# A diffusion step on one Trainium2 core: adaLN scale and shift brought into column form by small matmuls

## The reference

```python
def modulation(cvec, w_mod_l, b_mod_l):
    m = jax.nn.silu(cvec) @ w_mod_l + b_mod_l
    return m.reshape(cvec.shape[0], 6, D_MODEL)

def trunk_layer(x, mod, ...):
    sh1, sc1, g1, sh2, sc2, g2 = [mod[:, i][:, None, :] for i in range(6)]
    h = rms_norm(x, n1) * (1.0 + sc1) + sh1
    q, k, v, u = jnp.split(h @ w_in, ...)
    # QK norm, rotary on the sample, attention, and beside it
    # a Conformer module: gate, 31-tap convolution, layer_norm(z, ln_g, ln_b), silu
    x = x + g1 * (jnp.concatenate([attn, conv], axis=-1) @ w_out)
    h2 = rms_norm(x, n2) * (1.0 + sc2) + sh2
    x = x + g2 * grouped_moe(h2, ...)
```

## Time and profile before

| | us |
|---|---|
| median of 3 runs | 1169.36 (1165.12 to 1169.71) |
| profiled execution | 1165.68 |
| its span in the trace | 1163.8 |
| TensorE busy in it | 980.0 (84%) |
| VectorE busy | 407.9 (35%) |
| ScalarE busy | 158.2 (14%) |
| GpSimd busy | 116.8 (10%) |

### The profile page before, as it was taken

The page is one execution under the profiler, slowest core; times in us unless marked ns, Lnnn a source line. Parts: engine busy times, 40 slices in busy tenths (PEclk is TensorE's granted clock), DMA queues, the critical chain, the costliest instruction groups (busy, mean ns, idle before and its releaser), DMA issues.

```text
span 1163.8 us, 11201 instructions
## 1 busy us (share of the span) xinstructions
PE 980.0 (84%) x4106; PEld 443.5 (38%) x4106; DVE 407.9 (35%) x1072; ACT 158.2 (14%) x362; POOL 116.8 (10%) x164
## 2 busy tenths in 40 slices
PE   3589979999889988997839996999858997978890
PEld 0344525545333333333225553554523333333330
DVE  0019868733411111111042986954421111111113
ACT  0110123311000000000021023431100000000001
POOL 0100310230110000000030030041010000000001
PEclk8789979998989999998869997999769999998996
DMA  9934992348999987999975434034965999999805
GB/s 315 378 135 144 218 387 116 145 127 305 425 412 422 422 367 261 396 426 425 411 296 185 144 139 192 8 139 162 346 249 207 409 426 424 425 419 426 372 19 180
DMA packets 65412, 331.71 MB, mean 285 GB/s; under 512 B 6993, under 2 KB 9713, under 8 KB 48929
## 3 DMA queue, kind: packets, MB, share of 16 engines
q1 hardware_dynamic: 44224, 277.89, 59.9%
q10 hardware_dynamic: 12464, 23.79, 6.9%
q0 software_dynamic: 8624, 28.71, 6.8%
HBM read 308.25 MB, written 22.12 MB: 284 GB/s over the span
## 4 chain that ended last, share of the span: by engine, by line
PE 64%; DMA 19%; DVE 10%; issue 2%; ACT 2%; SPq 2%; POOL 1%; ACTq 0%; DVEq 0%; POOLq 0%
PE ps L1618 19%; PE ps L1327 15%; DMA big<-in_w_up_dram 10%; PE ps L1634 9%; PE ps L1534 7%; DVE scr L1000 4%; PE ps L1343 4%; DMA x<-in_x_sample_dram 2%; DMA big<-in_w_down_dram 2%; PE ps L1462 2%; DMA scr<-h_rows,slot_tok 1%; PE ps L1397 1%; DMA scr<-expert_rows,pick_y 1%; PE ps L1357 1%; PE ps L1602 1%
## 5 line engine op out<-in xcount | busy, mean ns | idle before, releaser
L1618 PE MATMUL ps<-big 128*64 128x512 f32 x1024 | 246.9, 633 | 41.3 <-DMA big<-in_w_up_dram 23.1
L1000 DVE SCALAR_TENSOR_TENSOR scr<-scr,convw 128x128 f32<-128x128 f32 (+1 forms) x480 | 160.5, 408 | 0.0
L1618 PEld LDWEIGHTS ps<-big 128*64 128x64 f32 x1024 | 82.0, 145 | 181.5 <-issue 167.4
L1634 PE MATMUL ps<-big,scr 128*64 128x512 f32 x624 | 146.3, 605 | 5.0 <-DVE scr L1290 4.3
L1327 PE MATMUL ps<-big 128*128 128x512 f32 (+1 forms) x384 | 146.1, 541 | 0.0
L1299 DVE TENSOR_TENSOR scr<-ps,scr 128x256 f32<-128x256 f32 x32 | 13.6, 425 | 309.9 <-ACT scr L873 309.9
L1343 PE MATMUL ps<-big,cs_rep 128*64 128x512 f32 x320 | 83.3, 667 | 22.0 <-DMA big<-in_w_mod_dram 22.0
L1327 PEld LDWEIGHTS ps<-big 128*128 128x128 f32 x384 | 72.9, 191 | 69.8 <-issue 67.5
L1534 PE MATMUL ps<-big 128*128 128x512 f32 x192 | 84.4, 594 | 1.4 <-ACT big L739 1.4
L1634 PEld LDWEIGHTS ps<-big,scr 128*64 128x64 f32 x624 | 49.8, 139 | 88.8 <-issue 88.3
L873 ACT ACTIVATE scr<-ps 128x256 f32<-128x256 f32 x32 | 12.3, 384 | 356.6 <-PE ps L1618 356.6
(11 more groups left out here) (198 smaller groups left out, 758.3 us busy)
## 6 DMA issues: line engine op xcount, KB each, us to landing
big<-in_w_gate_dram SPq DMA_DIRECT2D x32, 2048.0 KB, 15.5
big<-in_w_up_dram SPq DMA_DIRECT2D x32, 2048.0 KB, 20.6
big<-in_w_down_dram SPq DMA_DIRECT2D x32, 2048.0 KB, 18.0
big<-in_w_mod_dram SPq DMA_DIRECT2D x23, 2048.0 KB, 17.5
big<-in_w_in_dram SPq DMA_DIRECT2D x6, 2048.0 KB, 28.6
expert_rows<-scr ACTq DMA_DIRECT2D x78, 128.0 KB, 8.0
big<-in_w_out_dram SPq DMA_DIRECT2D x4, 2048.0 KB, 17.4
expert_rows<-x ACTq DMA_DIRECT2D x1, 6656.0 KB, 36.4
```

The lines of the kernel that those rows point to most:

```text
L1000: v.scalar_tensor_tensor(out, span, w, out, ALU.mult, ALU.add).then_inc(conv_step[part_], 1)
L1618: mm = pe.matmul(ps[b * TT:(b + 1) * TT, bank, :].rearrange("p (m n) -> p m n", m=2), tokens(k), w[:, :, k, b * HF:(b + 1) * HF], start=(k ...
L1634: mm = pe.matmul(ps[b * TT:(b + 1) * TT, bank, :], src[:, k % 2 * P + k // 2 * TT:k % 2 * P + (k // 2 + 1) * TT], w[:, k, b * SEG:(b + 1) ...
```

## The change

Vectors 0 and 1 are taken from PSUM by a plain copy, without bias or gain. Sixteen small matmuls for each vector turn the copied rows into columns in PSUM: the row block is the stationary operand (64 columns at a stride of eight numbers), two columns of the identity are the moving one. Bias and gain come from DRAM directly as columns (`colA`, 24 numbers for each partition), and VectorE adds and multiplies them on 16 numbers for each partition. Nothing of these two vectors goes through DRAM any more.

The order changes too. x is loaded between vectors 0 and 1; the piece that is loaded in two halves is now the last of vector 1. On TensorE, columns of vector 0 and the transposes of x tiles 0 and 1 stand between the two vectors. The layer norm rows have a semaphore of their own (`ln_in`); in layer 0 they are loaded after ScalarE's share of the first tiles. GpSimd waits for the columns before it clears the convolution's edges, since the copied rows now lie in the scratch space of `zT`.

```diff
-FIRST = ("v", 0, 0, 0)
+HALVED = ("v", 0, 1, 1)
...
-        rowA, gainA = scr[:, 5120:5120 + 2 * LW], scr[:, 5120 + 2 * LW:5120 + 3 * LW]
+        rowA = scr[:, 7168:7168 + 2 * LW]
+        colA = scr[:, 7168 + 2 * LW:7168 + 2 * LW + 3 * KD].rearrange("p (s k) -> p s k", k=KD)
...
-        def columns(eng, l):
-
-            eng.wait_ge(mod_done, 2 * l + 1)
-            lane_out(eng, mod_dram[:, 0:2 * D], rowA, modA_st[l])
-            eng.wait_ge(modA_st[l], 32)
-            for g_ in range(2):
-                eng.dma_start(modcol[:, g_], mod_dram[g_, 0:2 * D].rearrange("(s p k) -> p s k", s=2, k=KD))\
-                    .then_inc(modcol_in[l], 16)
...
             load_vector(0, 0)
-            load_vector(0, 1)
             sp.dma_start(x[:, 0, :], x_prompt[0]).then_inc(x_in, 16)
             sp.dma_start(x[:, 1:3, :], x_sample[0].rearrange("(t p) n -> p t n", p=P)).then_inc(x_in, 16)
+            load_vector(0, 1)
...
+                pool.wait_ge(cols_ready, l + 1)
                 g.memset(zT[:, :, 0:PAD], 0.0).then_inc(pads_set, 1)
...
+                    if t == 0:
+                        pool.wait_ge(ln_in, (l + 1) * 32)
                     pool.wait_ge(ln_norm, l * 3 + t + 1)
...
-                if l + 1 < LAYERS:
-                    columns(pool, l + 1)
...
-                lane_in(act, rowA, b_mod[l:l + 1, 0:2 * D], rowA_in)
-                lane_in(act, gainA, norm1_g[l:l + 1, :], rowA_in)
+                act.dma_start(colA[:, 0:2], b_mod[l, 0:2 * D].rearrange("(s p k) -> p s k", s=2, k=KD)).then_inc(colA_in, 16)
+                act.dma_start(colA[:, 2], norm1_g[l].rearrange("(p k) -> p k", k=KD)).then_inc(colA_in, 16)
...
-                if l == 0:
-                    columns(act, 0)
-                act.wait_ge(modcol_in[l], 32)
+                act.wait_ge(cols_ready, l + 1)
...
                     ins.then_inc(hTa_ready, 1)
+                if l == 0:
+                    ln_loads(0)
...
+                if c < 2:
+                    v.tensor_copy(rowA[:, c * LW:(c + 1) * LW], ps[:, bank, :]).then_inc(mod_taken, 1)
+                    return
...
+            def columns(l):
+
+                def taken(s_):
+                    return ps[:, 6 + s_, 0:2 * KD].rearrange("p (k g) -> p g k", g=2)
+
+                def over(n):
+                    return colA[:, n].unsqueeze(1).broadcast_to([P, 2, KD])
+
+                dve.wait_ge(colA_in, (l + 1) * 32)
+                dve.wait_ge(cols_ps, 2 * l + 1)
+                v.tensor_tensor(modcol[:, :, 0, :], taken(0), over(0), ALU.add)
+                dve.wait_ge(cols_ps, 2 * l + 2)
+                step.link(v.tensor_tensor(modcol[:, :, 1, :], taken(1), over(1), ALU.add))
+                v.scalar_tensor_tensor(modcol[:, :, 1, :], modcol[:, :, 1, :], 1.0, over(2), ALU.add, ALU.mult)\
+                    .then_inc(cols_ready, 1)
...
                 if l:
                     mod_take(l, 2)
+                    columns(l)
                     combine(l - 1, 0)
...
                     mod_take(0, 1)
+                    columns(0)
+                dve.wait_ge(cols_ready, l + 1)
                 for t in range(TILES):
                     take_hT(t)
...
+            def columns(l, s_):
+
+                pe.wait_ge(mod_taken, taken_at(l, s_))
+                for k in range(KD):
+                    for b in range(LANES):
+                        mm = pe.matmul(ps[b * LP:(b + 1) * LP, 6 + s_, 2 * k:2 * k + 2],
+                                       rowA[:, s_ * LW + k:(s_ + 1) * LW:KD], ident[:, b * LP:b * LP + 2],
+                                       start=True, stop=True)
+                mm.then_inc(cols_ps, 1)
...
             vector(0, 0)
-            vector(0, 1)
             pe.wait_ge(table_in, 16)
             pe.wait_ge(router_in, 32)
+            columns(0, 0)
+            x_transposed(0, 0)
+            x_transposed(0, 1)
+            vector(0, 1)
+            columns(0, 1)
             for l in range(LAYERS):
                 if l:
 
                     vector(l, 2)
                     pe.wait_ge(y_taken, l * E)
+                    columns(l, 0)
+                    columns(l, 1)
+                    x_transposed(l, 0)
+                    x_transposed(l, 1)
...
+                hT_first(0)
+                x_transposed(l, 2)
```

More of the change, by code:

```diff
@@ L326, in build @@
         rowB_in = sem("rowB_in"); gain_in = sem("gain_in"); small_in = sem("small_in")
-        modA_st = [sem(f"modA_st{l}") for l in range(LAYERS)]; modB_st = sem("modB_st"); modG_st = sem("modG_st"); rowC_in = sem("rowC_in")
-        modC_st = sem("modC_st"); rowG_in = sem("rowG_in"); rowA_in = sem("rowA_in")
-        bcA_in = sem("bcA_in"); modcol_in = [sem(f"modcol_in{l}") for l in range(LAYERS)]; bcG_in = sem("bcG_in")
+        modB_st = sem("modB_st"); modG_st = sem("modG_st"); rowC_in = sem("rowC_in")
+        modC_st = sem("modC_st"); rowG_in = sem("rowG_in"); colA_in = sem("colA_in"); cols_ps = sem("cols_ps"); cols_ready = sem("cols_ready"); ln_in = sem("ln_in")
+        bcA_in = sem("bcA_in"); bcG_in = sem("bcG_in")
         slot_loaded = [sem(f"slot_loaded{s}") for s in range(MOE_SLOTS)]
@@ L564, in _ @@
                 pool.dma_start(gainB, norm2_g[l:l + 1, :].broadcast_to([2, D])).then_inc(gain_in, 16)
-                pool.wait_ge(mod_done, 2 * l + 2)
+                pool.wait_ge(mod_done, l + 1)
                 lane_out(pool, mod_dram[:, 3 * D:4 * D], rowB, modB_st)
@@ L681, in small_loads, with ln_loads @@
                 act.dma_start(qkg[:, 1, :], k_norm_g[l:l + 1, :].broadcast_to([P, HD])).then_inc(small_in, 16)
-                act.dma_start(lnB[:, 0, :], conv_ln_g[l:l + 1, :].broadcast_to([P, CH])).then_inc(small_in, 16)
-                act.dma_start(lnB[:, 1, :], conv_ln_b[l:l + 1, :].broadcast_to([P, CH])).then_inc(small_in, 16)
+            def ln_loads(l):
+                act.dma_start(lnB[:, 0, :], conv_ln_g[l:l + 1, :].broadcast_to([P, CH])).then_inc(ln_in, 16)
+                act.dma_start(lnB[:, 1, :], conv_ln_b[l:l + 1, :].broadcast_to([P, CH])).then_inc(ln_in, 16)
             act.dma_start(table_sb[:, :], table).then_inc(table_in, 16)
@@ L824, in _ @@
                     small_loads(l + 1)
+                    ln_loads(l + 1)
                 for t in range(TILES):
@@ L911, in mod_take @@
                     dve.wait_ge(slot_used[slot_of(n)], uses(n))
+                if c < 2:
+                    v.tensor_copy(rowA[:, c * LW:(c + 1) * LW], ps[:, bank, :]).then_inc(mod_taken, 1)
+                    return
                 if c < 8:
-                    row, gain = (rowA[:, 0:LW], rowA[:, LW:2 * LW], rowC[:, :], rowB, None, rowG)[c], gainA
+                    row = (rowC[:, :], rowB, None, rowG)[c - 2]
                     v.tensor_tensor(row, ps[:, bank, :], row, ALU.add).then_inc(mod_taken, 1)
@@ L918, in mod_take @@
                     v.tensor_tensor(row, ps[0:2, bank, :], row, ALU.add).then_inc(mod_taken, 1)
-                if c in (1, 8, 9):
+                if c in (8, 9):
                     if c == 8:
@@ L1336, in vector @@
                     for k in range(max(a, k0), min(b, k1)):
-                        if n == FIRST and k == 0:
+                        if n == HALVED and k == a:
                             pe.wait_ge(first_half, 16)
-                        elif k == (2 if n == FIRST else a):
+                        elif k == (a + 2 if n == HALVED else a):
                             loaded(n)
@@ L1363, in head_fill, with x_transposed @@
                             mm.then_inc(slot_used[slot_of(n)], 1)
+            def columns(l, s_):
[6 more added lines that the diff above has]
+                mm.then_inc(cols_ps, 1)
+            def x_transposed(l, t):
+                pe.wait_ge(diag_ready, l * 3 + t + 1)
+                for n in range(2 * t, 2 * t + 2):
+                    for m in range(4):
+                        mm = pe.matmul(ps[:, n % 4, m * P:(m + 1) * P], x[:, t, 4 * (n % 2) + m::KD], diag[:, t, :],
+                                       start=True, stop=True)
+                    mm.then_inc(hT_ps, 1)
             vector(0, 0)
-            vector(0, 1)
             pe.wait_ge(table_in, 16)
             pe.wait_ge(router_in, 32)
+            columns(0, 0)
[3 more added lines that the diff above has]
+            columns(0, 1)
             for l in range(LAYERS):
@@ L1389, in hT_first @@
                     pe.wait_ge(hTd_ready, l * 3 + t + 1)
-                for t in range(TILES):
-                    pe.wait_ge(diag_ready, l * 3 + t + 1)
-                    if t == 2:
-                        hT_first(0)
-                    for n in range(2 * t, 2 * t + 2):
-                        for m in range(4):
-                            mm = pe.matmul(ps[:, n % 4, m * P:(m + 1) * P], x[:, t, 4 * (n % 2) + m::KD], diag[:, t, :],
-                                           start=True, stop=True)
-                        mm.then_inc(hT_ps, 1)
+                hT_first(0)
+                x_transposed(l, 2)
```

(2 more changed lines are left out.)

5 lines of the change are left out of this document (1 added, 4 removed).

## The result

The changed kernel takes 1156.01 us (median of 5 runs, 1154.12 to 1157.31) against 1169.36 us (5 runs, 1164.59 to 1169.71): a ratio of 0.9909, 95% interval 0.9885 to 0.9933. It is faster by 0.9%, and the time lies in the forecast range, 3.5 us under the value named. The profiled execution took 1154.12 us, 11.6 us less than the one before (11.5 by the spans in the trace); the forecast saving was 7.8. Between medians the difference is 13.4 us, by the ratio 10.6.

A forecast was written before the change was run, and what follows sets the result against it. The priced stretch, up to the first scaled tile, was bound by queued transfers, then DRAM trips. Saving 7.3 plus 0.5, 7.8 us, gave 1157.9 from the profiled execution, 1161.6 from the median; 1159.5 was named, range 1152 to 1168.

The forecast's parts named there:

- The main step: Start of the kernel: time from the first w_mod pieces to ScalarE's first scaled tile, forecast at 52.5 us instead of 59.79.
- Traffic at the start: Loads ahead of the first w_mod pieces: fewer bytes land vector 0's second piece 2.4 us sooner, at 20.7 us.
- Columns 0 (C): TensorE at the start, after vector 0: sixteen fp32 matmuls, 32 records at 0.131 us, take 4.2 us.
- The low bound, 1.9: Column matmuls of one vector: at 0.06 us a record, the load overlapping wholly, they take 1.9 us.
- the dear rival: Column matmuls: the strided 64-column load costs as much as 128 columns, 7.9 us a vector; 1170.6 us in all; chance 0.12.
- Vector 1: TensorE at the start, after x tiles 0 and 1: pure matmul, 8.0 us, ending at 46.8 us.
- The first projections: First 48 projection records: a smaller TensorE gap before tile 2 credits 0.5 us of a possible 0.74.
- What costs nothing: GpSimd's later memsets, later layer norm loads and layer 1's columns delay nothing; layer 1 is hidden by 1.3 us.
- A start that comes d us sooner should therefore move the whole rest by d: From the first projections to the end: everything comes earlier by one constant, the forecast saving of 7.8 us.

## Why the prediction came out as it did

The main step held: the work between the first w_mod pieces and the first scaled tile sets when the projections begin, and on chip it is TensorE's list in series. Its sizes were too dear, and one step failed: that a lead at the start moves the whole rest by as much.

- *Traffic at the start.* Forecast 2.4 us, from the low end of 2.1 to 3.8, on the ground that the layer norm rows were queued last. Vector 0 ended 2.9 us before the forecast 25.8; putting the traffic back cost 4.2 us at the landing. The whole 1280 KB at 307 GB/s, 4.3 us, fits that; no run puts back the layer norm rows alone.
- *Columns 0 (C).* Forecast 4.2, measured 2.09, twice: 4.2 us. The price of one strided load was right (0.122 against 0.123 to 0.153). What was missed is that the lanes alternate and overlap. The low bound, 1.9, was nearly reached, but not by the reason given for it: the stride isn't free, 0.065 against 0.029 contiguous. The 335 against 191 ns of the earlier trace rows was no sign of the stride either: with two moving columns and a granted clock of 0.50 the loads of 128 columns show a median of 335 ns strided and 333 contiguous. The Trainium skill, SBUF — State Buffer, section Door 1: The DMA port swizzle, on which the dear rival leaned, has each crossing of a 16-byte line pay; the trace agrees that stride costs (0.065 against 0.029, both on alternating lanes at the full clock) and shows that the strided time goes with the columns (0.122 for 64, 0.238 for 128), so the narrower load does halve it.
- *Vector 1.* Forecast 8.0, measured 7.09 without a wait: 0.9 us. Together 2.9 + 4.2 + 0.9 = 8.0 of the 8.3 us by which 44.16 beats 52.5.
- *The first projections.* Credit 0.5, measured 0.74 (21.34 to 20.60).
- *What costs nothing* held. GpSimd's memsets went at 44.19, and the two layer norm issues at 48.06 and 48.43 on ScalarE, with nothing late behind them. Layer 1's columns are hidden by 6.6 us, not 1.3.
- *"A start that comes d us sooner should therefore move the whole rest by d"* failed. The idle transfer engines at 230 us were checked, but not what the 32 added matmuls do to the instruction stream. Of 17 us of lead at expert 0, 5.1 went before expert 1, and after some ups and downs 11.5 arrived. It can go the other way: with 24 and 24 idle matmuls the lead at expert 0 is 15.5 us (316.35 to 300.81), and the profiled execution (1146.59) is 19.1 us under the one before. The forecast had named the test (the shift at the first projection found again at the end), and the test failed.

So it was in part luck that the value came out near: two errors of 8.3 and about 5 us had opposite signs.

That position makes the wait before expert 1 is shown: idle matmuls alone remove it, and put it into the kernel before. For the total it is shown one way only: idle matmuls made the changed kernel faster, and the kernel before not clearly slower. How position does it is argued, not shown. In the changed kernel an instruction packet begins to move between 311.5 and 312.0 us and TensorE goes on at 314.24; another between 342.0 and 342.5, and it goes on at 344.49. In the version with 24 and 24 idle matmuls the packets of this stretch come at 304.5 to 305 and 313.5 to 314, while matmuls run. At the end of each expert stands a conditional part (L485), which TensorE jumps over where the expert does not overflow. Behind it come two one-column matmuls (L1684, at 308.31), and only then the wait: the stall is not at the jump but some instructions after it. The Trainium skill, Runtime: NRT & Kernel Launch, section Instruction fetch mechanics, says that instructions come in blocks of 256, that a jump out of the two loaded blocks must wait for a fetch, and that the crossing of a block is mostly hidden. 256 agrees with 64 matmuls of four instructions; 5.69 us is not hidden. No run took the jump away, so whether it is the jump is open, as is why the same wait did not raise the time of the kernel before.

## What to carry to other kernels

Price small matmuls with a strided stationary operand by its columns, and let neighbours alternate between column halves of the array: a record went from 0.122 to 0.065 us, and cutting 128-column transposes the same way took a tile from 3.9 to 2.2 us at the full clock (3.5 at a granted clock of 0.54). When the number of matmuls ahead of a stage changes, look for new "issue" waits in that stage before the change itself is judged, and try a few positions with idle matmuls: here position was worth some 8 to 9.5 us, not much less than the change with its 10.6 to 13.4. A lead at the start is only worth what the trace still shows at the end, so follow it from stage to stage.

## What was not expected of the hardware

- Strided matmuls of 64 stationary and two moving columns overlap on alternating lanes: 0.065 us a record against 0.122 on one lane.
- A strided record of 128 columns takes 0.238 us even with two moving columns, at a granted clock of 0.50, where a contiguous one takes 0.216; and an x tile takes 3.9 us whether the granted clock is 0.61 or 0.73 on average.
- Moving the same instructions by 32 matmuls brought a wait of 5.40 to 6.05 us into the profiled execution of each kernel that had this shift, and moving them by 56 or 64 left 0.55 to 0.61.
